# Loading w_down with two neighbouring rows per partition in the expert loop of a hybrid decoder step

## What is computed

```python
D_MODEL, N_EXPERTS, TOP_K, D_FF = 1024, 32, 4, 1024

def moe(x2, w_router, b_router, w_gate_up, b_gate_up, w_down, b_down):
    logits = x2 @ w_router + b_router
    top_v, top_i = lax.top_k(logits, TOP_K)
    gates = jax.nn.softmax(top_v, axis=-1)
...
    def expert_block(args):
        xe, e = args
        gu = xe @ w_gate_up[e] + b_gate_up[e]
        gate, up = gu[:, :D_FF], gu[:, D_FF:]
        gate = jnp.minimum(gate, SWIGLU_LIMIT)
        up = jnp.clip(up, -SWIGLU_LIMIT, SWIGLU_LIMIT)
        h = gate * jax.nn.sigmoid(SWIGLU_ALPHA * gate) * (up + 1.0)
        return h @ w_down[e] + b_down[e]
...
    return jnp.sum(y * gates[..., None].astype(y.dtype), axis=1)
```

## Time and profile before

| | |
|---|---|
| median of 3 runs | 1377.25 us (1376.51 to 1377.64) |
| the profiled execution's own time | 1377.18 us |
| its span in the trace | 1375.0 us |
| TensorE (PE) busy | 1264.2 us, 92% |
| VectorE (DVE) busy | 830.7 us, 60% |
| ScalarE (ACT) busy | 615.9 us, 45% |
| weight queue of the DMA engines | 435.28 MB, 78.8% of 16 engines' span |
| gather and scatter queue | 21.33 MB, 6.4% |

### The profile page before, as it was taken

The page is one execution under the profiler, slowest core; times in us unless marked ns, Lnnn a source line. Parts: engine busy times, 40 slices in busy tenths (PEclk is TensorE's granted clock), DMA queues, the critical chain, the costliest instruction groups (busy, mean ns, idle before and its releaser), DMA issues.

```text
span 1375.0 us, 19053 instructions
## 1 busy us (share of the span) xinstructions
PE 1264.2 (92%) x6157; PEld 804.9 (59%) x6158; DVE 830.7 (60%) x1352; ACT 615.9 (45%) x828; POOL 141.0 (10%) x154
## 2 busy tenths in 40 slices
PE   7999999898989898989898998989898989898992
PEld 5888854483737464655556464737373737465860
DVE  3896667782837465564647373828282737565953
ACT  4111342562635454453626262726263635445832
POOL 8100020100010000001000000000001010000010
PEclk9999999898999999999999999999999999999997
DMA  9610275599999999999999999999999999999913
GB/s 320 83 36 1 90 268 244 180 305 412 409 390 411 395 417 399 400 417 397 414 392 415 381 414 386 418 391 413 390 410 389 409 378 414 379 394 410 374 22 130
DMA packets 83768, 457.02 MB, mean 332 GB/s; under 512 B 16012, under 2 KB 19524, under 8 KB 67352
## 3 DMA queue, kind: packets, MB, share of 16 engines
q1 hardware_dynamic: 72728, 435.28, 78.8%
q0 software_dynamic: 11008, 21.33, 6.4%
HBM read 440.52 MB, written 23.63 MB: 338 GB/s over the span
## 4 chain that ended last, share of the span: by engine, by line
PE 46%; DMA 24%; DVE 4%; issue 4%; ACT 2%; DVEq 0%; POOLq 0%; POOL 0%; ACTq 0%; SPq 0%
PE bank L2053 33%; DMA ymix<-ffn_in,idx_next 10%; DMA token_sums<-ymix,row_cur 8%; DMA ring_lo<-in_w_gate_up 4%; PE bank L2098 4%; PE bank L2109 4%; PE bank L2038 2%; DVE w_lo L2196 2%; DMA token_sums<-x 2%; ACT ymix L1945 1%; PE bank L2044 1%; ACT w_hi L1919 1%; PE bank L2060 0%; PE bank L2069 0%; DVE cmix L2217 0%
## 5 line engine op out<-in xcount | busy, mean ns | idle before, releaser
L2196 DVE TENSOR_TENSOR w_lo<-ring_lo,w_hi 128x1024 fp32r<-128x1024 f32 x271 | 315.0, 1220 | 84.0 <-ACT w_hi L1919 77.6
L1919 ACT ACTIVATE w_hi<-ring_lo 128x1024 fp32r<-128x1024 f32 x271 | 274.8, 1058 | 32.1 <-PE bank L2053 17.6
L2098 PE MATMUL bank<-ring_lo,x_s 128*64 128x512 f32 x1024 | 230.3, 597 | 0.0
L2053 PE MATMUL bank<-w_hi,x_hi 128*128 128x512 f32 x544 | 173.4, 400 | 2.5 <-issue 2.5
L2053 PE MATMUL bank<-w_lo,x_hi 128*128 128x512 f32 x544 | 168.7, 391 | 0.0
L2053 PE MATMUL bank<-w_hi,x_lo 128*128 128x512 f32 x544 | 168.3, 391 | 0.0
L2196 DVE TENSOR_TENSOR w_lo<-w_out,w_hi 128x1024 fp32r<-128x1024 f32 x136 | 160.0, 1218 | 0.4 <-ACT w_hi L1919 0.4
L2222 DVE TENSOR_SCALAR cmix<-bank 128x256 f32<-128x256 f32 x32 | 13.6, 425 | 239.6 <-ACT cmix L1978 239.6
L2098 PEld LDWEIGHTS bank<-ring_lo,x_s 128*64 128x64 f32 x1024 | 69.3, 137 | 127.4 <-issue 127.0
L1919 ACT ACTIVATE w_hi<-w_out 128x1024 fp32r<-128x1024 f32 x136 | 138.7, 1059 | 9.3 <-PE bank L2053 9.3
L2109 PE MATMUL bank<-w_out,h_s 128*64 128x512 f32 x512 | 137.8, 675 | 0.0
(11 more groups left out here) (423 smaller groups left out, 1402.5 us busy)
## 6 DMA issues: line engine op xcount, KB each, us to landing
ring_lo<-in_w_gate_up SPq DMA_DIRECT2D x128, 2048.0 KB, 13.4
w_out<-in_w_down SPq DMA_DIRECT2D x128, 1024.0 KB, 15.7
ring_lo<-in_w_in SPq DMA_DIRECT2D x3, 2048.0 KB, 20.7
w_out<-in_w_out SPq DMA_DIRECT2D x2, 2048.0 KB, 9.0
x<-in_x_prompt SPq DMA_DIRECT2D x6, 512.0 KB, 11.6
bias<-bias_rows SPq DMA_DIRECT2D x132, 3.0 KB
ring_lo<-in_w_in SPq DMA_DIRECT2D x2, 1024.0 KB, 11.1
token_sums<-x SPq DMA_DIRECT2D x4, 512.0 KB
```

The costliest lines, as they stand in the source:

```text
L1919: nc.scalar.activation(high(j), raw(j), ACT.Copy).then_inc(s["w_hi"], 1)
L2053: last = nc.tensor.matmul(bank[b + u][:], v[:, k, :], part(j)[:, u, :], start=(j == 16 and first), stop=(j in (7, 15, UNITS - 1) and part ...
L2098: last = nc.tensor.matmul(bank[2 * half][64 * u:64 * u + 64, :], x_s[:, k % 4, 64 * (k // 4):64 * (k // 4) + 64], gu[:, k, :, half, 256 * ...
L2196: v.tensor_tensor(low(j), raw(j), high(j).bitcast(F32), ALU.subtract).then_inc(s["w_lo"], 1)
```

## The change

Two things are changed together. A w_down load now takes the rows 256·b + 2·p and 256·b + 2·p + 1 for partition p (b is the number of the load, 0 to 3). These two rows lie side by side in device memory and in the buffer, so the instruction's form goes from 128x2x1024 to 128x2048: 8 KB in a row per partition, and half as many packets for the same bytes. The row that lies on partition p in piece k is therefore another one, so the transposes of h pick their columns accordingly: every second column, even ones for the first piece of a pair and odd ones for the second. The number of instructions on each engine, their order and their waits stay as they are.

```diff
     else:
         k = 2 * (j - 4)
-        src = a["w_down"][0].rearrange("e (k p) n -> e p k n", p=P)[e, :, k:k + 2, :]
+        src = a["w_down"][0].rearrange("e (b p t) n -> e b p t n", p=P, t=2)[e, j - 4]
         dst = mid["w_out"][:, k:k + 2, :]
     return eng.dma_start(dst, src)
...
         def h_transposes(q, half):
             pe.wait_ge(s["h"], 2 * q + half + 1)
             for k in range(4):
-                last = nc.tensor.transpose(bank[6 + half][:, k * P:(k + 1) * P], h_sb[:, k * P:(k + 1) * P], ident[:])
+                c = 2 * P * (k // 2) + k % 2
+                last = nc.tensor.transpose(bank[6 + half][:, k * P:(k + 1) * P], h_sb[:, c:c + 2 * P - 1:2], ident[:])
             last.then_inc(s["hT_psum"], 1)
...
             for c in range(2):
                 o = 256 * half + c * P
-                last = nc.tensor.transpose(bank[5][:, o:o + P], h_sb[:, o:o + P], ident[:])
+                last = nc.tensor.transpose(bank[5][:, o:o + P], h_sb[:, 256 * half + c:256 * half + 255 + c:2], ident[:])
             last.then_inc(s["hT_psum"], 1)
```

## The result

| | before | after |
|---|---|---|
| median | 1376.24 us (20 runs, 1374.51 to 1379.03) | 1379.45 us (20 runs, 1375.29 to 1384.01) |
| ratio after / before | | 1.0019, 95% interval 1.0011 to 1.0026 |
| profiled execution, its own time | 1377.18 us | 1379.41 us |
| its span | 1375.0 us | 1377.2 us |

The change made the kernel slower, by 0.19%, some 2.6 us by the ratio (the medians differ by 3.2 us): right at what can be told from no change, and on the other side from the forecast of 1373.2 us. The runs also lie further apart than those of before (8.7 us from lowest to highest, against 4.5).

A forecast was written before the change was run, and what follows sets the result against it. Bound by two nearly equal holders: the scatter-gather chain (64.9 us a pass plus clock) and late DMA engines (65.4 us). Terms: -5.2 + 1.2 + 0 = -4.0 us; 1375.0 - 4.0 + 2.2 = 1373.2 us, range 1364 to 1385.

The forecast's parts named there:

- two holders of nearly equal length: Expert loop: chain of scatter and gather, 64.9 us plus the clock's share, and late DMA engines, 65.4 us per pass.
- a few late engines: Some of the 16 DMA engines go from w_down into the next pass without rest; their work is 65.4 us.
- Price of a packet: w_down loads: an 8 KB packet takes 0.314 us against 0.328 for two of 4 KB, 0.014 us saved per pair.
- Relief of the late engines: w_down of two experts per pass: 0.88 us less work, from 65.4 to about 64.5 us.
- How much of it comes out? ... 5.2 us gained: Expert loop: the new pass taken as 65.0 us, 0.4 us x 13 = 5.2 us gained.
- The clock: TensorE after its stall runs at a lower clock for a while: up to 1.49 us a pass, 3 to 4 us either way.
- the one scatter of 8.49 us: Scatter when w_down had drained, against 9.1 to 9.2 us beside w_down packets; passes were to drift toward it.
- I charge nothing there, with 0 and 1.2 us as the ends: Wide block's scatter in later passes: waiting behind larger w_down packets costs nothing, as the late engines' bytes must go anyway.
- Rival 3: Small block, scatter's issue to gather's: scatter pays for larger packets every pass, up to 18 us, 1392 us; chance 0.15.
- Strided transposes: Weight loads of h's transposes reading every second column: 0 taken, 26.5 us on TensorE's path as the bad end.
- The first scatter: Scatter at 313.13, with w_down in full flow behind it: 1.2 us charged once for waiting behind larger packets.
- The page on descriptors: w_down packets: about 3 cycles overhead each, so 1.1% or 0.24 us saved of 20.9 us, some 3 us at most.

The follow-up runs named there:

- short turns for the gather: Two of four gate-and-up loads behind a small block in 8 KB instead of 16 KB packets: 1376.76 us on the kernel before, 1370.53 us on the changed kernel.
- the loads alone: New 8 KB w_down loads on the kernel before, with its old unit-stride transposes of h: 1378.08 us, ratio 1.0010.
- two groups of four: Eight traces of the kernels before, changed and partly changed, split by 4 KB (421.7 to 424.8 us) or 8 KB (427.1 to 428.1 us) w_down packets beside the scatter.
- two experiments with 8 KB packets there: On the kernel before: new w_down loads without strided transposes, 1378.08 us; both parts only for experts loaded behind a wide block, 1379.39 us.
- strides only: Transposes of h with column step two on the kernel before, with its old 4 KB w_down loads: 1377.23 us, ratio 1.0001.

## Why the prediction was wrong

*The range* of 1364 to 1385 us held the measured 1379.45. *The sign* did not: -4.0 us were forecast, +2.6 us came.

*What bounds the kernel* was read rightly in that it has two holders of nearly equal length. The short turns for the gather showed it: they bring nothing on the kernel before and about 9 us on the changed one (1379.45 to 1370.53 us). That the second holder is a few late engines was read from two windows and not tested.

*Price of a packet:* 0.313 us against 0.314 in a window of 1 us, but by the queue's total only 0.007 to 0.010 us are saved per pair, not 0.014. For the 64 pairs of a pass that is 0.4 to 0.7 us on an engine, against the 0.88 forecast. *Relief of the late engines:* 0.46 us per pass by the experiment, which fits this; half of the 0.88.

*"How much of it comes out? ... 5.2 us gained"* is the first step that failed in size. The mean pass was 65.38 - 64.90 = 0.48 us above the best one, 6.2 us over 13 passes, and 5.2 us of it were taken for late weights. The clock, which the prediction itself names as the second thing that lengthens passes, got no share. By the table, the 14 wide blocks of before stand 2.0 us above 14 of 35.13 us, and the stretches behind the stall 6.5 us above 14 of 5.66 us. So only some 2 us were there to be gained from late weights, and most of the excess was clock. In the wide block 1.8 us came out with the loads alone. The pass did not drift toward shorter scatters as I had taken from the one scatter of 8.49 us.

*"I charge nothing there, with 0 and 1.2 us as the ends"* is the step that turned the sign. The argument, that the late engines' bytes have to go in any case, holds for the mean scatter: it did not move. I had then treated a scatter whose mean stays as one that costs nothing. With turns twice as long it ranges over 1.8 to 2.9 us instead of 0.5 to 0.9, and the chain of scatter, stall and clock pays for that: some 4 us over 14 passes (427.5 us against 423.6 us, means of the two groups of four), against the 0 to 1.8 us gained in the wide blocks. Rival 3 named the place and the mechanism, the turn behind larger packets, but put it into every pass at its full price. With short turns for the gather, where the weights hold the pass, that is what came: about 1 us in every pass.

*The clock* stood beside all the cases as "3 to 4 us either way". It was no neutral term: the dear case came more than twice as often where the scatters vary. How a varying scatter leads to it was shown in part: a stall that was long by 0.5 us or more was often followed by it, but not always, and a short stall right behind such a pass always was. It came after ordinary stalls too (4.39 us at 727.11 before), and why it falls where it does stays open.

*Strided transposes:* charged 0; a weight load is 66 ns longer and a wide block 0.08 us, 1.2 us in all, too little to be seen in the times by itself. The upper end of 26.5 us was far off. The Trainium skill, page "SBUF — State Buffer", section "Door 1", would have had a step of two float32 at full bandwidth; here the trace does not agree: 206 ns against 140. That page speaks of the memory's lines, and why the load is longer was not tried.

*The first scatter:* 1.2 us charged; it took 9.95 us against 9.11, and the first stall was longer by 2.2 us in one profile of the changed kernel and 1.4 us in the other. But it varied from 6.3 to 7.2 us among the four traces with 4 KB packets beside the scatter, and it was 5.9 and 6.3 us in the two experiments with 8 KB packets there, so the packets do not settle it.

*The page on descriptors:* the Trainium skill's "DMA: Bandwidth & Descriptors", section "Why small descriptors are slow", gave 1.1% per pair of packets as an estimate; the windows of 1 us give 0.328 against 0.313 us, 4.6%, and the queue's total 0.007 to 0.010 of 0.328 us, 2 to 3%: more than the page's figure, and nearer to it than I had taken.

## What to carry to other kernels

Larger packets save time on the DMA engines, but each is also a longer turn for whatever shares the engines, so ask of every load what small transfer it flies beside, and whether somebody waits for that one. Where two holders are nearly equal, relieving one shows nothing or a small loss; the test is to relieve the other alone and then both. A term whose mean is zero can still cost, when what comes after it punishes delays more than it rewards gains. And before a gain is taken from what makes the mean pass longer than the best one, split that excess by cause.

## What the runs showed of the hardware

- In windows of 1 to 2 us a packet of 8 KB takes 0.313 us of a DMA engine, 4 KB 0.164 and 16 KB 0.615, near a straight line; over the whole weight queue, half as many w_down packets saved 0.007 to 0.010 us per packet less.
- A float32 weight load of 128 columns takes 140 ns with unit step and 205 to 207 ns with a step of two (strides only, and the changed kernel); its matmul's place in the stream moves by some 10 ns per transpose (0.08 us for eight).
- The weights' side of a pass needs 65.2 us with 8 KB and 65.7 us with 4 KB packets of w_down (short turns for the gather), though the DMA engines rest for part of it (in 778 to 779 before, the weight queue uses 6.5% of them).
- An accumulating scatter lasts longer where weight packets still go beside its end: 10.12 and 10.79 us with 11 and 9 of them in the window 6 us after its start, 8.21 and 7.89 us with none. Where the weights hold every pass, it takes about 10.1 us beside 8 KB packets and 9.1 us beside 4 KB packets.
- The same stall of 4.4 us can cost TensorE 1.5 us more or less in clock (granted 0.70 or 0.55 from its end to the wide block, after 531.73 and after 727.11 in the trace of before); what decides it was not found.
